# Root mean square norms applied behind the projections of both feed-forward stages and of q, k, v, on one Trainium2 core

## What is computed

```python
def rmsnorm(x, g):
    xf = x.astype(jnp.float32)
    var = jnp.mean(xf * xf, axis=-1, keepdims=True)
    return (xf * lax.rsqrt(var + RMS_EPS)).astype(x.dtype) * g
...
def conv_ffn(h, w_up, w_conv, w_down):
    gu = causal_dwconv(h @ w_up, w_conv)
    g, u = jnp.split(gu, 2, axis=-1)
    return (jax.nn.silu(g) * u) @ w_down
...
def second_block(x, ...):
    for i in range(DEPTH_2):
        h = rmsnorm(x, mix_norm[i])
        if i % N_MIXERS == 0:
            x = x + short_conv_mixer(h, sc_w_in[j], sc_w_conv[j], sc_w_out[j])
        else:
            x = x + moba_attention(h, moba_w_qkv[j], moba_w_o[j])
        x = x + conv_ffn(rmsnorm(x, ffn_norm[i]), ffn_w_up[i], ffn_w_conv[i], ffn_w_down[i])
    return rmsnorm(x, final_norm)
```

## Time and profile before

| | us |
|---|---|
| runs: median of 3 (lowest, highest) | 1138.96 (1138.21, 1139.0) |
| the profiled execution, its own time | 1140.76 |
| its span in the trace | 1138.9 |
| PE busy, share of the span | 1076.1, 94% |
| DVE busy | 842.6, 74% |
| ACT busy | 713.6, 63% |
| POOL busy | 76.3, 7% |
| mean granted clock of TensorE | 0.98 |

### The profile page before, as it was taken

One profiled execution on the slowest core, in us unless ns is written; L12 is line 12 of the kernel. 1 busy time (PEld: TensorE's weight loads), 2 busy tenths in 40 slices (PEclk: granted clock), 3 DMA queues, 4 the chain that ended last, 5 costly groups with the idle time before them and its releaser, 6 DMA issues.

```text
span 1138.9 us, 17179 instructions
## 1 busy us (share of the span) xinstructions
PE 1076.1 (94%) x6358; PEld 932.5 (82%) x6358; DVE 842.6 (74%) x1084; ACT 713.6 (63%) x947; POOL 76.3 (7%) x82
## 2 busy tenths in 40 slices
PE   7998979999999999889999999999899989999997
PEld 6877867777877787769988899998788868999996
DVE  5498678999899998767654776676867866766765
ACT  6667478888888887665433654454557765554553
POOL 1001100000000000030000110120000011101100
PEclk9999989999999999999999999999999998999999
DMA  9440528888889898645443545554343324555531
GB/s 369 163 161 25 212 82 306 332 333 316 343 320 343 312 352 305 243 157 185 170 168 143 186 173 197 188 185 179 148 148 111 111 96 151 203 198 189 185 142 38
DMA packets 33604, 232.62 MB, mean 204 GB/s; under 512 B 3856, under 2 KB 3984, under 8 KB 6032
## 3 DMA queue, kind: packets, MB, share of 16 engines
q1 hardware_dynamic: 32688, 229.98, 54.6%
q10 hardware_dynamic: 864, 1.93, 0.5%
HBM read 230.85 MB, written 1.05 MB: 204 GB/s over the span
## 4 chain that ended last, share of the span: by engine, by line
PE 78%; DVE 13%; ACT 4%; issue 3%; DMA 2%; POOL 1%; DVEq 0%; ACTq 0%; SPq 0%; POOLq 0%
PE bank L1862 11%; PE bank L1863 11%; PE bank L1864 11%; PE bank L2361 9%; PE bank L2362 9%; PE bank L2363 9%; DVE wlo L1104 5%; PE bank L2218 4%; PE bank L2219 4%; PE bank L2201 2%; DMA raw<-stream 1%; PE bank L2226 1%; PE bank L2267 1%; PE bank L2266 1%; DVE arena L1502 1%
## 5 line engine op out<-in xcount | busy, mean ns | idle before, releaser
L1104 DVE TENSOR_TENSOR wlo<-raw,whi 128x2048 fp32r<-128x2048 f32 x212 | 481.8, 2286 | 85.9 <-ACT whi L514 84.8
L514 ACT ACTIVATE whi<-raw 128x2048 fp32r<-128x2048 f32 x213 | 406.6, 1917 | 122.2 <-PE bank L2363 64.1
L2361 PE MATMUL bank<-xs,whi 128*128 128x256 f32 x896 | 252.2, 282 | 4.5 <-DVE wlo L1104 3.3
L2362 PE MATMUL bank<-xs,whi 128*128 128x256 f32 x896 | 251.3, 280 | 0.0
L2363 PE MATMUL bank<-xs,wlo 128*128 128x256 f32 x896 | 250.8, 280 | 0.0
L2361 PEld LDWEIGHTS bank<-xs,whi 128*128 128x128 f32 x896 | 169.5, 189 | 6.7 <-DVE wlo L1104 3.7
L2362 PEld LDWEIGHTS bank<-xs,whi 128*128 128x128 f32 x896 | 169.6, 189 | 0.8
L2363 PEld LDWEIGHTS bank<-xs,wlo 128*128 128x128 f32 x896 | 169.5, 189 | 0.0
L1862 PE MATMUL bank<-whi,rounded 128*128 128x512 f32 x344 | 139.3, 405 | 5.4 <-DVE rounded L1511 4.9
L1863 PE MATMUL bank<-wlo,rounded 128*128 128x512 f32 x344 | 137.7, 400 | 0.0
L1864 PE MATMUL bank<-whi,rounded 128*128 128x512 f32 x344 | 137.5, 400 | 0.0
(11 more groups left out here) (320 smaller groups left out, 1462.5 us busy)
## 6 DMA issues: line engine op xcount, KB each, us to landing
raw<-stream SPq DMA_DIRECT2D x215, 1024.0 KB, 4.8
arena<-finals ACTq DMA_DIRECT2D x3, 512.0 KB, 3.8
xres<-x_in SPq DMA_DIRECT2D x2, 512.0 KB, 5.0
raw<-stream SPq DMA_DIRECT2D x4, 256.0 KB, 6.2
out<-xn SPq DMA_DIRECT2D x4, 256.0 KB, 2.1
par<-params SPq DMA_DIRECT2D x1, 844.0 KB, 12.5
cst<-table SPq DMA_DIRECT2D x1, 502.0 KB, 8.9
arena<-p_in ACTq DMA_DIRECT2D x1, 256.0 KB, 6.0
```

The source lines that it names most:

```text
L514: act.activation(whi[:, s, :], raw[:, a, :], ACT.Copy).then_inc(S("high_done"), 1)
L1104: dve.tensor_tensor(wlo[:, s, :], raw[:, unit0 % RAW, :], whi[:, s, :].bitcast(F32), ALU.subtract)\
L2361: pe.matmul(o, whi[:, s, w], xhi[:, kk, :], start=first, stop=False, skip_group_check=True)
L2362: pe.matmul(o, whi[:, s, w], xlo[:, kk, :], start=False, stop=False, skip_group_check=True)
```

## The change

The root is no longer applied to the residual before the turn. PE turns the unscaled `xres` for norms 5, 6 and 7, and the root goes to the outputs:

- **Feed-forward stages.** Positions lie along the bank there, so PE makes a row of the roots on all partitions after group 0 (two matmuls of `rstd`, broadcast, by the identity, into bank 4), ACT copies it to `root_row`, and in every step DVE multiplies both banks by it into a new buffer `fraw` (two instructions of 128 by 512, semaphore `rooted`). ACT's first tap and DVE's eight taps then read `fraw` and not the banks, and the banks are free for the next group once `fraw` is written.
- **q, k, v.** POOL multiplies the rotation's tables by the roots into `trig` (four instructions), `rope` reads `trig`; `v_high` scales by the root, and `v_low` becomes a `scalar_tensor_tensor`.
- **Sums by column half.** The turn of column half 0 moves ahead of the last matmuls of the stage before; that of half 1 is cut in two, ahead of the next stage's first matmuls (tile 0) and between them (tile 1). The squares are summed behind the turns' copies. Banks of `down` are numbered by column half, and feed-forward 0's `last_down` goes column half by column half.
- **The group of the last step** (`halves_apart`) is done in two passes: both units for the first half of the hidden columns (`half_done`), then both again for the other half. `unit_used` rises in the second pass only.

```diff
@@ ffn_dve, and likewise by halves in ffn_last_dve
                 ahead(3)
+                dve.wait_ge(S("unit_used"), group_end(u0, e, e0))
+                if e0 == 0:
+                    dve.wait_ge(S("root_ready"), layer + 1)
+                for half in range(2):
+                    ins = dve.tensor_tensor(fraw[:, b, 2 * half:2 * half + 2, :],
+                                            bank[2 * gb + half][:].rearrange("p (f t) -> p f t", f=2),
+                                            root_row.unsqueeze(1).broadcast_to([P, 2, T]), ALU.mult)
+                ins.then_inc(S("rooted"), 1)
+                dve.wait_ge(S("rooted"), d0 + 1 + e)
                 dve.wait_ge(S("ffn_begun"), layer * FH + 1 + e)
...
@@ ffn_last_dve
                 split_to(u0 + 3 * FE - 1)
                 for half in range(2):
+                    dve.wait_ge(*((S("unit_used"), group_end(u0, e, e)) if half else (S("half_done"), layer + 1)))
+                    dve.tensor_tensor(fraw[:, b, half::2, :], bank[2 * gb + half][:].rearrange("p (f t) -> p f t", f=2),
+                                      root_row.unsqueeze(1).broadcast_to([P, 2, T]), ALU.mult)\
+                       .then_inc(S("rooted"), 1)
...
@@ the vector queue between the stages
+            split_to(U_SCOUT + 3)
+            add_first(C_SCOUT, CHUNK_END[C_SCOUT])
+            split_to(U_FFN0)
+            turn_dve(5, range(0, 4))
+            add_second(C_SCOUT, 5, 0)
+            split_to(U_FFN0 + 1)
+            add_second(C_SCOUT, 5, 1)
+            turn_dve(5, range(4, KD))
...
             ffn(0)
-            add_down(B_FFN0, 6, U_FFN0 + 3 * FE)
-            for t in range(TT):
-                normed(6, t)
-            turn_dve(6)
+            for t in range(TT):
+                dve.wait_ge(S("bank_done"), B_FFN0 + t + 1)
+                add(t, 0, 4 + t)
+            turn_dve(6, range(0, 4))
+            dve.wait_ge(S("bank_done"), B_FFN0 + 3)
+            add(0, 1, 6)
+            dve.wait_ge(S("unit_used"), U_FFN0 + 3 * FE)
+            add(1, 1, 7)
             split_to(U_QKV + 1)
+            turn_dve(6, range(4, KD))
...
+            split_to(U_FFN1)
             o_low(7)
-            add_chunks(U_WO, C_WO, 7, U_WO + 3, late=2)
-            turn_dve(7)
+            add_first(C_WO, U_WO + 3)
+            add_second(C_WO, 7, 0)
+            turn_dve(7, range(0, 4))
+            add_second(C_WO, 7, 1)
             split_to(U_FFN1 + 1)
+            turn_dve(7, range(4, KD))
...
@@ group
-                for i in range(2):
+                for part_, i in [(p, i) for p in range(2 if halves_apart else 1) for i in range(2)]:
                     s = wait_unit((unit0 + i, off))
...
-                        for at in range(4):
+                        if kk in ahead_of:
+                            ahead_of[kk]()
+                        for at in range(2 * part_, 2 * part_ + 2) if halves_apart else range(4):
...
-                    ins.then_inc(S("unit_used"), 1)
+                    if part_ or not halves_apart:
+                        ins.then_inc(S("unit_used"), 1)
+                    elif i:
+                        ins.then_inc(S("half_done"), 1)
...
@@ experts (the PE queue of a feed-forward stage)
-                group(g0, u0, q)
+                turn_tile(q, 0, range(4, KD))
+                group(g0, u0, q, ahead_of={2: lambda: turn_tile(q, 1, range(4, KD))})
+                pe.wait_ge(S("xt_ready"), KD * q + 2)
+                for t in range(TT):
+                    pe.wait_ge(S(f"rstd{t}_ready"), q + 1)
+                    ins = pe.matmul(bank[4][:, P * t:P * t + P], rstd[:, t:t + 1].broadcast_to([P, P]), ident,
+                                    start=True, stop=True, skip_group_check=True)
+                ins.then_inc(S("root_made"), 1)
...
+                    last_down((count - 1) % 2, u0 + 3 * count - 1, d0 + count,
+                              [(f, c, t) for c in range(2) for f in range(2) for t in range(TT)],
+                              lambda: [turn_tile(6, t, range(4)) for t in range(TT)])
...
@@ the norms on ACT
+            turn_act(7, range(0, 4))
+            norm_act(7, slice(0, 2))
+            turn_act(7, range(4, KD))
+            norm_act(7, slice(2, 4))
...
@@ q, k, v
+                    ins = pool.tensor_scalar(trig[:, n, t, :], src[:, HALF * t:HALF * t + HALF], rstd[:, t:t + 1], None,
+                                             ALU.mult)
+            ins.then_inc(S("trig_ready"), 1)
...
-                    ins = act.activation(vt[:, 0, t, 512 * half:512 * half + 512], out_bank(C_QKV + c, t)[:], ACT.Copy)
+                    ins = act.activation(vt[:, 0, t, 512 * half:512 * half + 512], out_bank(C_QKV + c, t)[:], ACT.Copy,
+                                         scale=rstd[:, t:t + 1])
```

More of the change, by code:

```diff
@@ L811, in ffn_last_act @@
                 for half in range(2):
+                    act.wait_ge(S("rooted"), d0 + 1 + e + half)
                     for f in (half, 2 + half):
-                        ins = act.activation(facc[:, b, f, :], bank[2 * gb + half][:, (f // 2) * T:(f // 2 + 1) * T],
-                                             ACT.Copy, scale=cwn[:, b, 8 + f:9 + f])
+                        ins = act.activation(facc[:, b, f, :], fraw[:, b, f, :], ACT.Copy,
+                                             scale=cwn[:, b, 8 + f:9 + f])
                     ins.then_inc(S("ffn_begun"), 1)
@@ L1124, in normed, with turn_dve @@
                        .then_inc(S(f"xn{t}_ready"), 1)
-            def turn_dve(q):
-                for k in range(KD):
+            def turn_dve(q, ks=range(KD)):
+                for k in ks:
                     if k % 2 == 0:
@@ L1396, in _ @@
             turn_y_dve(2)
-            add_chunks(U_WOUT, C_WOUT, 1, U_WOUT + 3, late=True)
+            split_to(U_WOUT + 4)
+            add_first(C_WOUT, U_WOUT + 3)
+            dve.wait_ge(S("final_loaded"), 16)
+            for t in range(TT):
+                tokens_scaled(t, 0)
+            for t in range(TT):
+                add_second(C_WOUT, 1, t)
+                tokens_scaled(t, 1)
             turn_dve(2)
@@ L1864, in mm3, with turn_tile @@
                 return pe.matmul(o, al, bh, start=False, stop=stop, skip_group_check=True)
-            XN_TURNS = (4, 5, 6, 7)
+            XN_TURNS = (4,)
+            def turn_tile(q, t, ks):
+                for k in ks:
+                    if k % 4 == 0:
+                        pe.wait_ge(S(f"residual{t}_ready"), 2 * q - 1 + k // 4)
+                    ins = pe.transpose(turned_k(q, k)[:, P * t:P * t + P], xres[:, t, P * k:P * k + P], ident)
+                    if t == 1 and k % 2:
+                        ins.then_inc(S("turned"), 1)
             def turn(q):
@@ L1922, in dense @@
                     ins.then_inc(S("unit_used"), 1)
+                    if u == 0 and between:
+                        between()
             pe.wait_ge(S("ident_loaded"), 16)
@@ L2555, in _ @@
             o_part(1, 1, (2, 3), (0,))
+            for t in range(TT):
+                turn_tile(7, t, range(4))
             o_part(1, 1, (2, 3), (1,))
-            turn(7)
             experts(G_FFN1, FH, U_FFN1, FE, 7)
```

182 lines of the change are left out of this document (88 added, 94 removed).

## The result

The changed kernel takes 1147.11 us (median of 4 runs, 1146.09 to 1149.23), the kernel before 1138.59 (4 runs beside it, 1136.59 to 1139.0): ratio 1.0075, 95% interval 1.0048 to 1.0101. The prediction was 1143.4, in a range from 1136.5 to 1148.5, with 0.63 for slower by over 0.2%. Slower it is, by 8.5 us and not by 4.4. The profiled execution took 1146.09, its span is 1144.3.

The account below looks back on a forecast made before the run. The prediction took PE to bound the kernel (78% of the last-ending chain). Its terms, -4.4 - 7.9 + 4.2 + 0.8 + 7.8 - 0.7 + 4.6, gave +4.4 us on 1138.96: 1143.4, range 1136.5 to 1148.5.

Parts of the forecast that it names:

- The pauses that go: PE's pauses ahead of the two feed-forward stages vanish: -4.4 us into feed-forward 0, -7.9 into feed-forward 1.
- First step: First step of each feed-forward stage: PE pauses 3.7 us instead of 1.6, +2.1 twice.
- Group 10: Group 10 in two passes wants its second unit sooner than the split ends: +0.4 us twice.
- Last step: Last step of each feed-forward stage: late split ahead of both multiplies, PE pauses 4.3 us, +3.9 twice.
- Ahead of q, k, v: From feed-forward 0's last product into q, k, v: a gain of 0.7 us.
- Steady steps: Middle feed-forward steps: DVE's added multiplies stay hidden, with 1.1 us to spare each round.
- rival 3: DVE becomes the bound of the steady steps, each of 20 losing 0.5 us: +10 more, 1153; chance 0.09.
- rival 4: Taps reading SBUF are shorter, 0.5 us in each of four chains, 2.0 in all: 1141.4; chance 0.07.
- Clock: PE's clock falls behind the four new long pauses, losing 0 to 1.7 us each: +4.6 in all.
- rival 1: The new pauses come but the clock does not fall: -0.2 us, 1138.8, no change; chance 0.2.
- a pause of 1.9 at once cost none: Profile row ahead of q, k, v: PE's 1.9 us pause left the clock at 1.00.
- Rival 2: Last step costs nothing if its split's slot is freed about 5 us before the group's end: 1133.1; chance 0.12.

Follow-up runs that it names:

- experiment 1: Changed kernel with the last unit's split moved late, behind the first half's copies on ACT and the second half's multiply on DVE: 1137.54 us.
- experiment 3: Changed kernel with 37 unread matmuls of 128x256 added on PE ahead of each feed-forward stage's last product: 1145.82 us.
- experiment 2: Changed kernel with group 10 in one pass and both multiplies behind the group's end: 1143.3 us.
- experiment 5: Changed kernel with DVE's pair of multiplies done twice in steps 1 to 9, the extra pair written where nobody reads: 1152.93 us.
- experiment 4's second run: Kernel before the change, with group 1's second unit split ahead of the taps in each feed-forward first step: 1134.26 us.
- experiment 4: Group 1's second unit split early in each feed-forward first step: 1151.17 us in the changed kernel, 1134.26 us in the kernel before.
- experiment 9: Changed kernel with both ends of feed-forward stages reordered, DVE's tile 0 add ahead of splitting turned blocks, and the rotation's table scaled on ACT: 1123.95 us.

## Why the prediction came out as it did

**The pauses that go** (-4.4, -7.9). Both went. With the +2.1 of the first step the prediction had -2.3 and -5.8. Measured -3.45 and -5.39; but the kernel before had half speed behind its pause at 584, and the changed kernel's execution had none there. The late split, which did, needs 46.86 us for the stretch, so like with like it is -1.9. Right within half a microsecond, twice.

**First step** (PE pauses 3.7): 3.67 and 3.68. Right.

**Group 10** (+0.4): 0.40 twice. Right, though its working (8.7 against 8.4) gives 0.3.

**Last step** (PE pauses 4.3, +3.9): 4.35 twice, 4.1 more than the 0.24 before. Bringing it down to 0.5 gave 3.9 (experiments 1 and 3). The reason was right too: the split ahead of both multiplies, more than the late slot, which is 1.4 of it (experiment 2).

**Ahead of q, k, v** (-0.7): -0.5, as far as the clock stays up. One reason in it was wrong. The prediction had POOL's four multiplies done some 2 us before the rotation, which was to wait for DVE's splits, 22.9 us behind the last product's start. In experiment 1, where that start is at 795.24, the rotation began at 22.8, but it waited for POOL last, 0.6 us beyond the splits; the two came out that close by luck:

```profile
812.39 5.56 POOL L1104 TENSOR_SCALAR trig<-cst,rstd 128x32 f32<-128x32 f32 x4
...
818.05 0.42 DVE L1762 TENSOR_TENSOR arena<-bank,trig 128x256 f32<-128x256 f32 x1 [0.59 <-POOL trig L1104]
```

**Steady steps** (1.1 us to spare, rival 3 if hand-overs cost more): over 1.3 (experiment 5). The 1.1 counted only the time behind the third split; the same working leaves DVE idle for another 1.1 ahead of it, from 12.3 to 13.4. Rival 3 did not happen.

**Taps from SBUF** (rival 4). The changed kernel's taps read SBUF and take 479 ns each, against 476 from the bank:

```profile
L1672 DVE SCALAR_TENSOR_TENSOR arena<-arena,cwn 128x255 f32<-128x255 f32 x80 | 33.4, 479 | 37.6 <-ACT arena L795 37.6
```

The 65 ns less for each tap, the prediction's estimate from the Trainium skill's VectorE: DVE Perf Modes, "The TRN2 errata", do not show in this row. Where page and row differ, the row decides.

**Clock** (+4.6): this is the term that was too small, by 4.0 us. "Between 0 and 1.7 each" took its upper end from a single row, 3.9 us at 0.56 behind a pause of 2.1. The last of these rows already had a longer pause, of 3.9 us ahead of the turns for feed-forward 1, and the clock at 0.50 for all of its 3.0 us; it breaks off before the clock rises, at about 946.5. Behind the four new pauses the windows show 5.8, 5.9, 3.1 and 4.5 us at about 0.5 with PE busy. In the table that is 2.8 of the +7.30 (the rest, 4.5, is the wait of 0.40 and the pause's 4.1) and 1.6 of the +6.16; ahead of q, k, v it is 2.0, and at the end 2.2. Together 8.6, where the term had 4.6. Put in its place the sum makes +8.4; measured 8.5. That these two are so close is partly luck: by the stretches the other terms came out about 1.4 worse than predicted (0.4 in each of the two stretches ahead of a first step, 0.2 in each last step, 0.2 ahead of q, k, v), and the half speed at 584, which only the kernel before had in its profiles, hides 1.5 of it. That each of the four pauses would be followed by half speed is what the Trainium skill, TensorE: Matmul & The Clock Gate, in "What's actually happening", has by default without activity, and the four windows agree; how much of it falls into busy time is what these rows had to show, and the row that the prediction went by was too short for it. Without this term the sum is -0.2, the result of rival 1. So the changed kernel is slower mainly by what the clock does behind its new pauses. This is not the clock's whole account: what the kernel before loses at half speed ahead of its two feed-forward stages (0.9 us, and 1.8 by the clock until 946.5) is inside the -4.4 and the -7.9.

The other row under that term, "a pause of 1.9 at once cost none", was no rule either. It cost none in both executions of the kernel before, but not in experiment 4's second run.

**Rival 2** (the last step costs nothing, decided by when the slot comes free) named the wrong condition. The slot came no earlier in experiment 1 and PE paused 0.5: it is decided by what stands ahead of the first half's multiply in DVE's queue.

## What to carry to other kernels

A step that is moved behind a product joins the chain of the next hand-over. Look at the first and the last step of a loop, where no other product covers that chain, and put work that merely prepares the next operand behind what PE waits for, or ahead of where the engine would stand idle. Ahead of moving a split on one engine, look at what the other engine's half of it stands behind (experiment 4). As an estimate from this kernel, price a pause of PE of some 4 us at its length and half as much again for the clock: taking away the two of 4.35 us gave 3.9 us of length each, and 2.0 and 2.2 of clock; behind the two of 3.7 us the stretches show 2.8 and 1.6 of clock.

## What the runs showed of the hardware that was not expected

- Behind pauses of the same length (3.67 and 3.68) PE ran 5.6 us at half speed in feed-forward 0's first step and 3.1 in feed-forward 1's, in both executions of the changed kernel. What decides between the two was not tried.
- Behind the same pause of 2.07 us, at the short convolution's output, the clock fell in both executions of the kernel before and in neither of the changed kernel's; in experiments 1 to 3, whose instructions up to there are the changed kernel's, it fell. So the changed kernel's two profiles may be the exception here, and its stretch of 45.35 us 1.5 us shorter than in its other executions; the two traces can't tell. The work ahead of it, with the same instructions in all variants, ends between 581.4 and 586.7 us, and two profiles of one kernel agree far better (584.30 and 584.12; 581.39 and 582.83). A difference of 3 us between two kernels' single profiles therefore need not come from the instructions that were changed; what brings it about is open.
- POOL's copies of twelve taps take 5.7 us each in the changed kernel, 2.1 in the one before, though source and target are the same. The line in the changed kernel:

```profile
L1084 POOL COPY cwn<-par 128x12 f32 x16 | 92.0, 5749 | 177.0 <-DVE arena L1672 177.0
...
L1104 POOL TENSOR_SCALAR trig<-cst,rstd 128x32 f32<-128x32 f32 x4 | 5.6, 1410 | 0.1
```

  No engine waited for the copies. The four pieces of the table, though, 5.6 us on POOL, were what the rotation waited for last, 0.6 us; on ACT that wait is gone (experiment 9). Why the copies got slower stays open.
